# Gate/up tiles 4 to 15 of both feed-forward blocks by seven block products, with the sums of weight blocks made by accumulating transfers

## The reference

```python
def swiglu(h, w_gate, w_up, w_down):
    return (jax.nn.silu(h @ w_gate) * (h @ w_up)) @ w_down
...
h = layer_norm(DN_ALPHA * h + 0.5 * swiglu(h, ffn1_w_gate[i], ffn1_w_up[i], ffn1_w_down[i]), ...)
h = layer_norm(DN_ALPHA * h + token_mixer(h, ...), ...)
h = layer_norm(DN_ALPHA * h + 0.5 * swiglu(h, ffn2_w_gate[i], ffn2_w_up[i], ffn2_w_down[i]), ...)
```

## Time and profile before

| | us |
|---|---|
| median of 3 runs (lowest, highest) | 1041.13 (1039.52, 1042.09) |
| the profiled execution, its own time | 1039.09 |
| its span, first to last instruction | 1037.3 |
| PE busy in the span | 970.1 (94%) |
| DVE / ACT / POOL busy | 760.3 (73%) / 494.8 (48%) / 52.1 (5%) |

### The profile page before, as it was taken

One profiled execution on the slowest core, in us unless ns is written; L12 is line 12 of the kernel. 1 busy time (PEld: TensorE's weight loads), 2 busy tenths in 40 slices (PEclk: granted clock), 3 DMA queues, 4 the chain that ended last, 5 costly groups with the idle time before them and its releaser, 6 DMA issues.

```text
span 1037.3 us, 17455 instructions
## 1 busy us (share of the span) xinstructions
PE 970.1 (94%) x7131; PEld 693.6 (67%) x7131; DVE 760.3 (73%) x1344; ACT 494.8 (48%) x707; POOL 52.1 (5%) x96
## 2 busy tenths in 40 slices
PE   2999999999999999999997899899899999999995
PEld 1888888888788886875565437665566644434584
DVE  6877766577987676877567978878777667889634
ACT  5576655244422245763335752567666434342214
POOL 0000000000020000000000010001000000011000
PEclk9999999999999999999998989999999999999999
DMA  5233322233334300212111012122332322424002
GB/s 210 84 111 122 114 91 94 77 109 120 112 119 152 123 2 1 82 42 71 52 41 42 1 35 88 49 74 82 123 122 88 117 82 82 163 99 170 15 1 82
DMA packets 24993, 89.26 MB, mean 86 GB/s; under 512 B 3035, under 2 KB 5427, under 8 KB 24915
## 3 DMA queue, kind: packets, MB, share of 16 engines
q1 hardware_dynamic: 23904, 87.17, 24.6%
q10 hardware_dynamic: 1011, 0.99, 0.3%
HBM read 86.05 MB, written 2.10 MB: 85 GB/s over the span
## 4 chain that ended last, share of the span: by engine, by line
PE 57%; DVE 25%; ACT 10%; issue 5%; DMA 2%; POOL 1%; SPq 0%; ACTq 0%; DVEq 0%
PE PS L732 9%; PE PS L682 9%; PE PS L758 8%; PE PS L853 7%; PE PS L652 6%; DVE cmax L1793 5%; PE PS L760 4%; DVE wsp L1815 4%; PE PS L763 3%; ACT wsp L1295 2%; PE PS L827 1%; DVE big L2020 1%; ACT H L1289 1%; PE PS L1133 1%; PE PS L976 1%
## 5 line engine op out<-in xcount | busy, mean ns | idle before, releaser
L652 PE MATMUL PS<-xs,wsp 128*128 128x264 f16 (+1 forms) x1344 | 195.4, 307 | 5.6 <-DVE wsp L1815 4.5
L652 PEld LDWEIGHTS PS<-xs,wsp 128*128 128x128 f16 x1344 | 131.0, 98 | 68.9 <-DVE wsp L1815 7.9
L732 PE MATMUL PS<-xs,wsp 128*128 128x264 f16 (+1 forms) x864 | 130.9, 310 | 0.0
L1793 DVE TENSOR_REDUCE cmax<-stage 128x1 f32<-128x2048 f32 (+2 forms) x47 | 120.2, 2557 | 4.5 <-DMA stage<-in_w_out 3.6
L1295 ACT ACTIVATE wsp<-stage,wscale 128x2048 f16<-128x2048 f32 (+2 forms) x34 | 70.8, 2081 | 100.0 <-DVE wscale L1779 78.1
L732 PEld LDWEIGHTS PS<-xs,wsp 128*128 128x128 f16 x864 | 84.5, 98 | 39.9
L2681 POOL PARTITION_ALL_REDUCE call<-cmax x73 | 48.8, 669 | 894.8 <-DVE cmax L1793 652.4
L1815 DVE SCALAR_TENSOR_TENSOR wsp<-stage,wscale,wsp 128x2048 f16<-128x2048 f32 (+2 forms) x34 | 83.3, 2449 | 12.8 <-ACT wsp L1295 12.8
L758 PE MATMUL PS<-big,arena 128*128 128x264 f16 (+1 forms) x792 | 89.4, 274 | 0.0
L758 PEld LDWEIGHTS PS<-big,arena 128*128 128x128 f16 x792 | 77.5, 98 | 11.5
L763 PE MATMUL PS<-big,wsp 128*128 128x264 f16 x660 | 75.1, 276 | 1.4 <-DVE big L2020 1.3
(11 more groups left out here) (267 smaller groups left out, 1421.8 us busy)
## 6 DMA issues: line engine op xcount, KB each, us to landing
stage<-in_gate SPq DMA_DIRECT2D x44, 512.0 KB, 3.7
stage<-in_up SPq DMA_DIRECT2D x44, 512.0 KB, 4.5
stage<-in_down SPq DMA_DIRECT2D x32, 704.0 KB, 5.3
stage<-in_w_in SPq DMA_DIRECT2D x16, 512.0 KB, 4.6
stage<-in_w_out SPq DMA_DIRECT2D x8, 512.0 KB, 4.2
X<-in_x SPq DMA_DIRECT2D x4, 512.0 KB, 6.2
out_T<-H SPq DMA_DIRECT2D x16, 128.0 KB, 1.7
stage<-in_w_in SPq DMA_DIRECT2D x2, 576.0 KB, 4.8
```

Of the source, the lines that this page charges most:

```text
L652: return nc.tensor.matmul(dst, w, x, start=k == 0 and wp + xp == 0, stop=k == KD - 1 and xp == 1)
L732: mm = nc.tensor.matmul(dst, w, x, start=k == 0 and wp + xp == 0, stop=k == KD - 1 and xp == 1)
L1793: nc.vector.tensor_reduce(cmax[:, one], stage[:, slot, 0:cols], AX.X, ALU.max, apply_absolute_value=True).then_inc(w_max, 1)
```

## The change

All twelve tiles 4 to 15 of each block are now done by the seven-product scheme; the pairs, and the functions for the plain odd tile, are gone. The activation sums change sign in two places, and the up result is scaled by a negated factor (`up_scale`), so that all four weight sums are additions.

The weight sums are no longer made by DVE. For each of the twelve tiles SP loads the chunk (gate, up: 1 MiB) and also loads up once more and the second half of gate into an area of its own (`sums_at`, 0.75 MiB). Then POOL issues four transfers of 128 x 512 float32 (256 KiB) from SBUF to SBUF that add onto what stands at the destination: first T1 += B11 and T3 += B22, then T2 += T1, then T4 += T2, each next one after the landing of the one that it reads. ACT's `weight_sum` of a tile now waits for the first two.

There are three buffers for chunks (the two stage slots and a new one) and three for split operands. The load of a chunk for tile m waits for the low parts of tile m-3's chunk (`raw_ready`) and its second sum; the load of its sums area waits for tile m-3's last split (`w_ready`). In the second block, and before tile 4's loads, SP waits until the layer norm ahead of the block is done (`x_ready`).

ACT and DVE split a tile in two parts: the four blocks that lie in the chunk (`raw_split_hi`, `raw_split_lo`, 2048 wide) and the three in the sums area (`sums_split_hi`, `sums_split_lo`, 1536 wide).

```diff
-SEVEN_AT = [4, 6, 8, 10, 12, 14]
+SEVEN_AT = list(range(4, 16))
+SUMMED = range(3, 18)
+N_BUF = 3
...
+            def load_seven(f, m):
+                i = m - SEVEN_AT[0]
+                if i == 0:
+                    if f == 0:
+                        sp.wait_ge(tok_sq, N_TOK)
+                    else:
+                        sp.wait_ge(x_ready, ln_tile(2, 2 * KD))
+                elif i < N_BUF:
+                    sp.wait_ge(w_ready, GU[f] + i + 2)
+                else:
+                    sp.wait_ge(raw_ready, seven(f, m - N_BUF) + 1)
+                    sp.wait_ge(t_second, 16 * (seven(f, m - N_BUF) + 1))
+                done = seven_loaded[buf(m)]
+                sp.dma_start(raw(f, m)[:, 0:KD * P], gate[f][m]).then_inc(done, 16)
+                sp.dma_start(raw(f, m)[:, KD * P:GU_COLS], up[f][m]).then_inc(done, 16)
+                if N_BUF <= i < 2 * N_BUF:
+                    sp.wait_ge(s_ready2, 4 * f + 4)
+                elif i >= 2 * N_BUF:
+                    sp.wait_ge(w_ready, GU[f] + m - N_BUF + 1)
+                sp.dma_start(sums_at(m)[:, 0:KD * P], up[f][m]).then_inc(done, 16)
+                sp.dma_start(sums_at(m)[:, KD * P:12 * P], gate[f][m][:, 4 * P:KD * P]).then_inc(done, 16)
...
+                for m in range(2, 4):
+                    if m == 3:
+                        load_seven(f, SEVEN_AT[0])
+                    sp.wait_ge(w_ready, GU[f] + m - 1)
+                    load_gu(f, m, (GU[f] + m) % 2)
+                for m in SEVEN_AT[1:]:
+                    load_seven(f, m)
...
                 for m in SEVEN_AT:
                     seven_first(f, m)
-                    gu_part(f, m + 1, 0)
                     seven_second(f, m)
-                    gu_part(f, m + 1, 1)
...
             def weight_sum(f, m):
...
+                if m in SEVEN_AT:
+                    act.wait_ge(t_first, 32 * (seven(f, m) + 1))
...
                 for m in SEVEN_AT:
-                    last = m == SEVEN_AT[-1]
-                    up_hi(f, m + 1)
...
+                    if m + 1 < SEVEN_END:
+                        raw_split_hi(f, m + 1)
...
                     p1_copy(f, m)
+                    if m > SEVEN_AT[0]:
+                        seven_gate(f, m - 1, 1)
+                    if m + 1 < SEVEN_END:
+                        sums_split_hi(f, m + 1)
+                    if m + 3 in SUMMED:
+                        weight_sum(f, m + 3)
                     hidden_sum(f, m - 1)
...
                     seven_gate(f, m, 0)
...
+                    if m > SEVEN_AT[0]:
+                        product_sum(f, m - 1, 3)
+                    scale_only(m + 2)
+                    if m + 1 < SEVEN_END:
+                        raw_split_lo(f, m + 1)
...
+                    if m > SEVEN_AT[0]:
+                        seven_hidden(f, m - 1)
+                    out_scale_only(m + 1)
                     product_sum(f, m, 0)
...
                     product_sum(f, m, 1)
                     product_sum(f, m, 2)
...
+                    if m + 1 < SEVEN_END:
+                        sums_split_lo(f, m + 1)
...
+            def first_sums(f, m):
+
+                quarter = blocks(raw(f, m))
+                pool.wait_ge(seven_loaded[buf(m)], seven_loads(f, m))
+                pool.dma_start(quarter[:, T1, :], quarter[:, B11, :], accum_op=ALU.add).then_inc(t_first, 16)
+                pool.dma_start(blocks(sums_at(m))[:, T3 - N_RAW, :], quarter[:, B22, :], accum_op=ALU.add).then_inc(t_first, 16)
...
+            def second_sum(f, m):
+
+                pool.wait_ge(t_first, 32 * (seven(f, m) + 1))
+                pool.dma_start(blocks(sums_at(m))[:, T2 - N_RAW, :], blocks(raw(f, m))[:, T1, :], accum_op=ALU.add).then_inc(t_second, 16)
...
+                    m = c - GU[f]
+                    if m in SEVEN_AT:
+                        first_sums(f, m)
+                    if SEVEN_AT[0] + 1 < m <= SEVEN_END:
+                        third_sum(f, m - 1)
                     over_all(c)
+                    if m in SEVEN_AT:
+                        second_sum(f, m)
```

More of the change, by code:

```diff
@@ L399, in build @@
         w_sum = sem("w_sum")
[L400 to L404, removed]
+        seven_loaded = [sem(f"seven_loaded{i}") for i in range(N_BUF)]
+        t_first = sem("t_first")
+        t_second = sem("t_second")
+        t_third = sem("t_third")
+        raw_hi = sem("raw_hi")
+        raw_ready = sem("raw_ready")
         s_added = sem("s_added")
@@ L521, in summed @@
         def summed(c):
-            return any(GU[f] + SUMMED_FROM <= c < GU[f] + PAIR_END for f in range(2))
+            return any(c - GU[f] in SUMMED for f in range(2))
         def sums_through(c):
@@ L531, in maxima_through, with loads_through, seven_loads, buf @@
             return c + 1 - sums_through(c)
+        def loads_through(c):
+            return 32 * sum(all(i - GU[f] not in SEVEN_AT for f in range(2)) for i in range(c % 2, c + 1, 2))
+        def seven_loads(f, m):
+            return 64 * (N_SEVEN // N_BUF * f + (m - SEVEN_AT[0]) // N_BUF + 1)
+        def buf(m):
+            return (m - SEVEN_AT[0]) % N_BUF
+        def raw(f, m):
+            return raw_third if buf(m) == 0 else stage[:, f if buf(m) == 1 else 1 - f, 0:GU_COLS]
+        def sums_at(m):
+            row = 6 + 3 * (m - SEVEN_AT[0]) if m < SEVEN_AT[0] + N_BUF else 15 + 3 * buf(m)
+            return big[:, row * T:row * T + 3 * 4 * P]
+        def blocks(ap):
+            return ap.rearrange("p (i n) -> p i n", n=4 * P)
         def by_half(f, ap):
@@ L560, in _ @@
             for f in range(2):
-                for m in range(2):
-                    if f:
+                if f:
+                    for m in range(2):
                         sp.wait_ge(w_ready, GU[f] + m - 1)
                         load_gu(f, m, (GU[f] + m) % 2)
[L565 to L568, removed]
+                for m in range(2, 4):
[5 more added lines that the diff above has]
+                    load_seven(f, m)
+                for m in range(SEVEN_END, KF):
+                    if m < SEVEN_END + 2:
+                        sp.wait_ge(raw_ready, seven(f, m - 2) + 1)
+                        sp.wait_ge(t_second, 16 * (seven(f, m - 2) + 1))
+                    else:
+                        sp.wait_ge(w_ready, GU[f] + m - 1)
+                    load_gu(f, m, (GU[f] + m) % 2)
                 for n, q in enumerate(DN_ORDER):
@@ L1338, in gate_hi @@
[L1338 to L1350 removed]
+                act.wait_ge(t_first, 32 * (g + 1))
@@ L1884, in gate_lo @@
[L1884 to L1896 removed]
+                w = seven_w[buf(m)]
```

248 lines of the change are left out of this document (94 added, 154 removed).

## The result

The changed kernel takes 1141.91 us (median of 4 runs, 1137.87 to 1145.63), the kernel before 1041.61 us on the same chip: a ratio of 1.0964, 95% interval 1.0912 to 1.1015. The profiled execution took 1137.87 us, its span is 1136.1 us, 98.8 us over that of before. The direction was forecast, the size was not: 28.7 us more were worked out, and the range ended at 1113 us.

A forecast was written before the change was run, and what follows sets the result against it. PE, busy 94%, bounds the kernel before; after, the ring makes it wait: 259.2 + 2 x 5.4 + 2.6 = 272.6 us of stages against 243.9, 28.7 us more, so 1070 us; range 1034 to 1113 us.

The forecast's parts named there:

- PE's work, 15.2 us less: On PE, six plain tiles per block become seven-product tiles: 8.1 + 7.1 = 15.2 us less.
- The ring through five engines: Chain from tile m's last split through loads, POOL, ACT and DVE to tile m+2's: 16.2 us + A per two tiles.
- two loads, 4.3 us: SP's loads of 512 and 256 KB into the sums area, taken to land 4.3 us after issue.
- A = 5.4 us: Time for POOL's two first sums to be issued and landed; forecast case 3.6 to 7.5 us, chance 0.52.
- 14 A - 46.9: The whole change in us as a function of A, breaking even at A = 3.35 us.
- I add 0.5 us: Allowance within A for POOL issuing the first sums while the next tile's chunk is being loaded.
- One of the signs of being wrong: PE's gaps would end on SP's loads taking twice as long as now because the transfer engines are full.
- The third rival: Transfer engines become the bound, 12.1 us per tile with destinations read too: 65 us more, 1106 us; chance 0.24.
- The two ends: Stage ends: one A, 5.4 us, charged per stage for the empty ring at its first tile, plus tile 3's 2.6 us.
- Tile 3's 2.6 us: Second block: PE waits 2.6 us for tile 3's split, its loads going out behind tile 4's.
- The second and third sums add nothing: On POOL and ACT, these sums have a whole tile more before ACT needs them, so nothing was added.
- PE's clock, taken as unchanged at 1.00: In the stages, PE was read at full granted clock, 1.00, and everything else was taken as unchanged.

The follow-up runs named there:

- The kernel with the later sum and less traffic: The change with two sums on DVE, absolute sum half a tile later, scale last, second block's tile 3 loads first: 1029.33 us, 0.9865 of before.
- Order alone: The change with absolute sum later on ACT, scale and second sum earlier on DVE and POOL, all transfers kept: 1071.10 us, 1.0254 of before.
- a shorter chain with all additions kept: The change without the second loads into the sums area for tiles 10 to 15 of each block: 1105.52 us, 1.0585 of before.
- no adds: The change without the four adding transfers of each tile, loads, splits and products kept: 1041.75 us, 1.0003 of before.
- thinning the traffic without it: The change with second and third sums made by DVE and 0.25 MiB loaded into the sums area, not 0.75: 1073.98 us, 1.0282 of before.
- the run without the all-reduce: The change with POOL making the additions itself and a 128 x 1 addition replacing the all-reduce in tiles 4 to 15: 1088.60 us, 1.0430 of before.

## Why the prediction was wrong, step by step

- **PE's work, 15.2 us less: right.** The kernel with the later sum and less traffic gives back 14.3 us in the stages.
- **The ring through five engines: the mechanism right, two terms too small.** Order alone took 71 us off, and a shorter chain with all additions kept took 2.9 us off each of the twelve tiles that it touched. The steps on ACT and DVE came within 0.5 us. The terms that failed are "two loads, 4.3 us", which took 7.1, and "A = 5.4 us", which took 7.4 in the turn shown. On average over twelve turns the loads' step, with SP's issue, was 8.4 us for 4.5, and A 6.8 for 5.4: this A lies inside the forecast's own 3.6 to 7.5 us, and with it alone 14 A - 46.9 would give 48 us, still inside the range. The term that broke the range is the loads.
- **Why those terms failed.** Both came from rows of a kernel whose transfer engines were 0.28 busy. Here they are 0.76 busy in the stages, and the loads of a tile's sums area, the next chunk's loads, the first sums and the third sum start within 8.4 us of each other (151.17 to 159.54). "I add 0.5 us" for that was the only allowance, and it was put on A and not on the loads. The bounds were given for A alone; the loads' 4.3 us stood in the sum as if known, so that even 9 us of A, the high end, gave only 1120 us. One of the signs of being wrong named them, loads that take twice as long as now because the engines are full: from issue to the last landing they took 6.6 to 9.1 us in the twelve turns, 7.7 on average, 1.8 times the 4.3, and the engines were not yet full.
- **The third rival was not an alternative to the forecast but a part of it.** Its 12.1 us per tile is near the 11.3 that the queues' shares give, but as a bound it can only show once the ring is opened. Short of full, the traffic had already lengthened each transfer of the ring, and the ring of latencies under load (13.4 us per tile) was slower than the 11.1 us that are left once it is opened.
- **The two ends: sizes wrong.** Tile 3's 2.6 us was right (3.15). The starts cost 13.3 us together, as 2A + 2.6 said, by chance: 3.8 in the first block and 9.5 in the second. The end of each stage was left out: the plain tiles 16 and 17 go back to two slots, and ACT waits 5 to 6 us for each of their loads even without additions.
- **"The second and third sums add nothing": right for the change** to within 13.3 us in all (L1389 waited in four places), wrong once the ring is opened (35.7 us in 18 places).
- **PE's clock, taken as unchanged at 1.00: wrong, but not a term of its own.** It was granted 0.89 and 0.88 of its higher level (2.4 GHz) in the stages after waits of 3 to 7 us, and the same matmuls took 256.7 us of PE where they took 228.4 with no adds. Most of this busy time lies where PE would else have waited for the ring: in the turn shown no step from 165.67 to 176.90 waits for PE. In three of the twelve turns p1_copy did wait for PE, 1.4 to 2.3 us (as at 154.87 and 208.67), and the steps on ACT and DVE took 12.6 to 13.4 us there. What the clock costs in all was not tried apart.

## What to carry to other kernels

When a change moves work onto the transfer engines, price every transfer in the chain at the load that the change itself makes, the old loads as well as the new transfers; a sum of latencies read at a busy share of 0.28 came out too low at 0.76. A wait on a transfer in an engine's ordered list costs what stands behind it: moving the absolute sum by half a tile, with the scale and the second sum that go with it, was worth 71 us, and thinning the traffic without it 68. With the additions kept on transfers, only both made PE the bound again.

## What the runs showed of the hardware

- An adding transfer of 256 KiB within SBUF took 1.5 us of all 16 engines and 144 packets (13824 / 96) in the change, a plain copy 0.70 us and 80 packets in the run with plain copies; both are worked out from the shares of the packets' time.
- Loads of 512 KiB into the sums area landed after a median of 3.7 us with no transfers of POOL's beside them, 4.6 with plain copies, 6.3 with additions.
- In the run in which POOL adds itself, POOL lost 5.95 us ahead of an all-reduce and 7.14 us ahead of a first addition (means of 26 each), some 13 us per tile; the trace has two records MODIFY_POOL_CONFIG of POOL at the start of each of these idles. The Trainium skill, GPSIMD Engine Reference, section 2.1 Instruction dispatch, names some 6 us for the first call of a freshly loaded kernel; the idles here agree in size, at every switch.
- In the run without the all-reduce, DVE's instructions with two operands in SBUF could stand still while POOL added in SBUF: a 128 x 1 product of scales (L2044) went from a median of 159 ns in the change to 1105 ns. The product sums (L1923), with one operand in PSUM, kept their 0.42 us. The Trainium skill, SBUF — State Buffer, section SBUF: two separate sides, has the two share a port that one holds for a whole instruction, and the rows agree.
